# Norm operands built from a gained copy of x, the low parts shared by VectorE and GpSimd

## The reference

```python
def rmsnorm(x, g):
    x32 = x.astype(jnp.float32)
    y = x32 * lax.rsqrt(jnp.mean(x32 * x32, axis=-1, keepdims=True) + EPS)
    return (y * g.astype(jnp.float32)).astype(x.dtype)

for i in range(DEPTH):                       # first block
    h = rmsnorm(x, norm_mix[i])
    x = x + (conformer_conv(h, ...) if i % 2 == 0 else dilated_attention(h, ...))
    h = rmsnorm(x, norm_ffn[i])
    x = x + swiglu(h, w_gate[i], w_up[i], w_down[i])

# second block, both layers: h = _rms_norm(x, norm)*(1+sc)+sh; x = x + g1*(mixer(h) @ w_out)
#                            h = _rms_norm(x, norm)*(1+sc)+sh; x = x + g2*swiglu(h, ...)
```

## Time and profile before

| | |
|---|---|
| time, median of 3 runs | 1299.03 us (1295.66 to 1299.97) |
| the profiled execution | 1299.97 us, of which its span is 1298.6 us |
| PE busy | 1206.4 us, 93% |
| DVE busy | 947.4 us, 73% |
| ACT busy | 659.1 us, 51% |
| POOL busy | 72.9 us, 6% |
| mean granted TensorE clock | 0.976 |

### The profile page before, as it was taken

How to read it: one execution, slowest core, us unless ns; L and a number is a source line. 1 busy time by engine, 2 the same in 40 slices (tenths; PEclk the granted TensorE clock), 3 DMA queues, 4 the chain that set the end, 5 groups by cost and what they waited for, 6 DMA issues and landing times.

```text
span 1298.6 us, 24598 instructions
## 1 busy us (share of the span) xinstructions
PE 1206.4 (93%) x9796; PEld 1149.0 (88%) x9796; DVE 947.4 (73%) x1813; ACT 659.1 (51%) x1142; POOL 72.9 (6%) x82
## 2 busy tenths in 40 slices
PE   5988899999998999999987879999999879999999
PEld 5957899999987999999976758999999767999999
DVE  5966598868777888888796658988885555776652
ACT  6326554445445644446455556444444766544431
POOL 1000000001000100003000011000010112000000
PEclk9999899999999999999998989999999989999999
DMA  8587698778863587778643225877875423555551
GB/s 280 164 193 106 217 306 256 257 261 273 266 184 114 183 270 258 238 269 268 204 147 104 86 93 179 273 253 252 263 261 195 135 90 98 181 187 184 181 193 66
DMA packets 81125, 259.35 MB, mean 200 GB/s; under 512 B 8904, under 2 KB 20424, under 8 KB 81012
## 3 DMA queue, kind: packets, MB, share of 16 engines
q1 hardware_dynamic: 81012, 257.79, 62.3%
HBM read 252.68 MB, written 5.08 MB: 198 GB/s over the span
## 4 chain that ended last, share of the span: by engine, by line
PE 69%; DVE 17%; ACT 5%; issue 4%; DMA 1%; POOL 1%; DVEq 0%; ACTq 0%; POOLq 0%
PE ps L516 63%; DVE wlo L1192 5%; DVE CV L1198 1%; DVE HL L1198 1%; DVE aacc L1198 1%; PE ps L576 1%; DMA raw<-wall 1%; DVE X L1198 1%; ACT oS L834 1%; ACT HH L834 1%; PE ps L607 1%; ACT eS L834 1%; ACT tmp L834 1%; PE ps L615 1%; DVE tmp L1523 1%
## 5 line engine op out<-in xcount | busy, mean ns | idle before, releaser
L516 PE MATMUL ps<-HH,whi 128*128 128x256 f32 (+1 forms) x2152 | 624.2, 290 | 28.4 <-DVE wlo L1192 11.8
L516 PE MATMUL ps<-HH,wlo 128*128 128x256 f32 (+1 forms) x2152 | 614.2, 285 | 0.0
L516 PE MATMUL ps<-HL,whi 128*128 128x256 f32 (+1 forms) x2152 | 613.6, 285 | 0.0
L834 ACT ACTIVATE whi<-raw 128x1024 fp32r<-128x1024 f32 x363 | 381.8, 1057 | 350.0 <-PE ps L516 342.7
L1192 DVE TENSOR_TENSOR wlo<-raw,whi 128x1024 fp32r<-128x1024 f32 x363 | 441.5, 1221 | 44.2 <-ACT whi L834 43.9
L516 PEld LDWEIGHTS ps<-HH,whi 128*128 128x128 f32 x2152 | 414.4, 193 | 46.3 <-issue 29.6
L516 PEld LDWEIGHTS ps<-HL,whi 128*128 128x128 f32 x2152 | 414.4, 193 | 0.9 <-issue 0.5
L516 PEld LDWEIGHTS ps<-HH,wlo 128*128 128x128 f32 x2152 | 413.9, 192 | 0.0
L516 PE MATMUL ps<-GH,whi 128*128 128x256 f32 x704 | 198.1, 281 | 0.6 <-DVE bcol L1405 0.5
L516 PE MATMUL ps<-GH,wlo 128*128 128x256 f32 x704 | 197.5, 281 | 0.0
L516 PE MATMUL ps<-GL,whi 128*128 128x256 f32 x704 | 197.5, 281 | 0.0
(11 more groups left out here) (209 smaller groups left out, 955.2 us busy)
## 6 DMA issues: line engine op xcount, KB each, us to landing
raw<-wall SPq DMA_DIRECT2D x363, 512.0 KB, 4.3
araw<-ada SPq DMA_DIRECT2D x96, 512.0 KB, 4.7
UR<-uscr SPq DMA_DIRECT2D x24, 142.0 KB, 3.3
scratch<-bvec SPq DMA_DIRECT2D x1, 3072.0 KB
oBB<-kbias SPq DMA_DIRECT2D x16, 192.0 KB, 2.6
aTB<-scratch SPq DMA_DIRECT2D x12, 128.0 KB, 2.3
X<-x_in SPq DMA_DIRECT2D x2, 512.0 KB, 5.8
out<-X SPq DMA_DIRECT2D x8, 128.0 KB, 3.0
```

Of the source, the lines that this page charges most:

```text
L516: ins = pe.e.matmul(o, l, r, start=(kt == p.order[0] and i == 0), stop=(kt == p.order[-1] and i == 2))
L834: ac.then_inc(ac.e.activation(o, i, func, **kw), sem)
```

## The change

The product of X and the gain is now written to memory once. DVE computes it as a tensor_scalar into one of three buffers `tn` right after it has updated X (function `gained`, counted by the new semaphore `xg`). ACT rounds that buffer to HH instead of scaling X itself. The low part is `HL <- tn - HH`, a tensor_tensor: on DVE for tiles 0, 2, 4, 6 and 7 (counter `hlv`), on POOL for tiles 1, 3 and 5 (counter `hlp`). DVE's low part stands in the same slot as the X update, where before it stood one slot later. ACT's squares wait for `xg` as well. PE waits for HH and for the counter of the engine that makes the tile's low part.

```diff
-NORM_OF = {1: "pw2", 2: "dn0", 3: "outd", 4: "dn1", 5: "oute", 6: "dn2", 7: "outo"}
+POOL_LOW = (1, 3, 5)
+LOW_NO = {0: 1, 2: 2, 4: 3, 6: 4, 7: 5, 1: 1, 3: 2, 5: 3}
...
+        def norm_low(i, nt):
+            return (S.hlp, 3 * i + LOW_NO[nt]) if nt in POOL_LOW else (S.hlv, 5 * i + LOW_NO[nt])
...
 (PE)            def ready(kt):
-                    pe.wait_ge(S.hl, 8 * i + kt + 1)
+                    pe.wait_ge(S.hh, 8 * i + kt + 1)
+                    pe.wait_ge(*norm_low(i, kt))
...
 (ACT)       def norm_high(i, nt):
-                streamed(i, nt)
+                ac.wait_ge(S.xg, 8 * i + nt + 1)
                 if i:
                     ac.wait_ge(S.mm, end_mm(HH_BEFORE[i]))
-                if i >= 4:
-                    ac.wait_ge(S.gn, 3 if i < 6 else i - 2)
-                act(HH[NORM_SET[i]][:, nt, 0:T], X[:, nt, :], ACT.Copy, S.hh, scale=gain(i, nt))
+                act(HH[NORM_SET[i]][:, nt, 0:T], TN[(8 * i + nt) % 3][:, :], ACT.Copy, S.hh)
             def square(i, nt):
-                streamed(i, nt)
+                ac.wait_ge(S.xg, 8 * i + nt + 1)
...
 (ACT)       def convolution():
-                ac.wait_ge(S.vec, 16)
...
 (DVE)
-            def norm_low(i, nt):
-                dv.wait_ge(S.hh, 8 * i + nt + 1)
-                stt(HL[NORM_SET[i]][:, nt, 0:T], X[:, nt, :], gain(i, nt), HH[NORM_SET[i]][:, nt, 0:T].bitcast(F32),
-                    ALU.mult, ALU.subtract, S.hl)
+            def gained(i, nt):
+                n = 8 * i + nt
+                if n >= 3:
+                    dv.wait_ge(S.hh, n - 2)
+                    dv.wait_ge(*norm_low(*divmod(n - 3, 8)))
+                if i >= 4:
+                    dv.wait_ge(S.gn, 3 if i < 6 else i - 2)
+                ts(TN[n % 3][:, :], X[:, nt, :], gain(i, nt), None, ALU.mult, None, S.xg)
+
+            def norm_lows(i, nt):
+                if nt not in POOL_LOW:
+                    dv.wait_ge(S.hh, 8 * i + nt + 1)
+                    tt(HL[NORM_SET[i]][:, nt, 0:T], TN[(8 * i + nt) % 3][:, :], HH[NORM_SET[i]][:, nt, 0:T].bitcast(F32),
+                       ALU.subtract, S.hlv)
...
 (DVE residual)
                     lows(low_to(name, nt))
-                    if i is not None and nt:
-                        norm_low(i, nt - 1)
                     ps = ended(name, nt)
...
                     stt(X[:, nt, :], ps[:, 0:T], scale(nt), X[:, nt, :], op, ALU.add, S.ev)
+                    if i is not None:
+                        dv.settle()
+                        gained(i, nt)
+                        norm_lows(i, nt)
...
 (DVE convolution)
                 for kt in range(KD):
-                    norm_low(0, kt)
+                    dv.wait_ge(S.x1 if kt >= 4 else S.x0, 16)
+                    gained(0, kt)
+                    norm_lows(0, kt)
...
 (POOL)
+            def norm_lows(i, nt):
+                if nt in POOL_LOW:
+                    po.wait_ge(S.hh, 8 * i + nt + 1)
+                    tt(HL[NORM_SET[i]][:, nt, 0:T], TN[(8 * i + nt) % 3][:, :], HH[NORM_SET[i]][:, nt, 0:T].bitcast(F32),
+                       ALU.subtract, S.hlp)
             def residual(name, i):
                 for nt in range(PROD[name].tiles):
+                    norm_lows(i, nt)
                     added(i, nt)
...
+            for kt in range(KD):
+                norm_lows(0, kt)
             for kt in range(KD):
                 added(0, kt)
```

More of the change, by code:

```diff
@@ L339, in __init__ @@
         self.hi, self.lo, self.mm, self.ev = new("hi"), new("lo"), new("mm"), new("ev")
-        self.hh, self.hl = new("hh"), new("hl")
+        self.xg, self.hh, self.hlv, self.hlp = new("xg"), new("hh"), new("hlv"), new("hlp")
         self.sq, self.sqa, self.tot = new("sq"), new("sqa"), new("tot")
@@ L400, in program @@
         TMP = [sb(f"tmp{i}", [P, T]) for i in range(9)]
-        TN = [sb(f"tn{i}", [P, T]) for i in range(2)]
+        TN = [sb(f"tn{i}", [P, T]) for i in range(3)]
         TS = [sb(f"ts{i}", [P, T]) for i in range(2)]
@@ L436, in program @@
             eBB = [sb(f"eBB{i}", [P, 384], F32, st) for i in range(2)]
-        eOB, eTD = TN, TS[0]
+        eOB, eTD = TN[0:2], TS[0]
         SQC, SQD = sb("SQC", [P, T]), sb("SQD", [P, T])
@@ L1293, in residual @@
                     else:
-                        dv.wait_ge(S.hl, 8 * j + nt + 1)
+                        dv.wait_ge(S.xg, 8 * j + nt + 1)
                     stt(X[:, nt, :], ps[:, 0:T], scale(nt), X[:, nt, :], op, ALU.add, S.ev)
+                    if i is not None:
+                        dv.settle()
+                        gained(i, nt)
+                        norm_lows(i, nt)
                     turned_sums(name, nt)
-                if i is not None:
-                    norm_low(i, p.tiles - 1)
             def convolution():
@@ L1636, in slot @@
                             dv.wait_ge(S.sq2, kt + 1)
-                            dv.wait_ge(S.hl, 8 * 4 + kt + 1)
                             stt(X[:, kt, :], X[:, kt, :], V("fin", kt), RST[0][:, :], ALU.mult, ALU.mult, S.xf)
```

## The result

The changed kernel took 1312.85 us (median of 4 runs, 1306.43 to 1316.91) beside 1299.5 us for the kernel before: 1.0102 times as long, 95% interval 1.0055 to 1.0149. A second set of runs beside the experiments gave 1310.67 us and 1.0098 (1.0075 to 1.0121). Forecast were 1305.4 us and 1300.5 to 1310. The direction was right, the size was not: +6.3 forecast, +11 to +13 measured. The profiled execution took 1311.96 us, its span is 1310.6 us, its mean granted clock 0.971 against 0.976.

The account below looks back on a forecast made before the run. PE was taken to bound the kernel, waiting at products' ends for DVE's last X updates. Start +2.8 and projections +3.5 gave +6.3 us, 1305.4 us for a run like the median; range holding 8 in 10: 1300.5 to 1310.

Parts of the forecast that it names:

- the price of each piece: Whole kernel: DVE's added busy time, +7.9 us, costs nothing in the dn products and everything after them.
- rival 3: Projections' ends: PE's stops grow to 3 us and more, the clock falls, POOL's low parts cost DVE; 1310 us, chance 0.14.
- The projections' +3.5: Ends of pw2, outd, oute, outo: later last X updates, added in full to PE's stops; 2.2 to 5.1 us, middle 3.5.
- the case with all of POOL's work paid by DVE: Projections: POOL's low parts shut out DVE's weight units, some 3 x 0.5 us more a projection; also within rival 3.
- 0.1 a slot: Projections: allowance of 0.1 us a slot for DVE's tensor_scalar being held up by POOL.
- The start: Norm 0: tn, HH and HL delay the squares, reciprocal at 31.2 instead of 28.40; +2.8 us, bounds +2.0 to +3.6.
- rivals 1 and 2: Start and projections: same, start hidden, 1301 to 1303 us, chance 0.19; faster, no POOL interference, 1296 us, chance 0.07.

Follow-up runs that it names:

- e15: The kernel before with only the norms of dn0 and dn1 made the changed way: 1300.11 us, 0.9998 of before.
- e1: The kernel before with only the norm built while dn2 runs made the changed way: 1303.08 us, 1.0024 of before.
- e6: The changed kernel with dn2's last nine modulation steps spread over 17 weight units instead of 13: 1307.11 us, 1.0051 of before.
- e7: The kernel before with dn2's last nine modulation steps spread over 17 weight units instead of 13: 1297.38 us, 0.9974 of before.
- e12: The kernel before with three idle tensor_scalars on DVE ahead of the X update of oute's tile 7: 1302.57 us, 1.0020 of before.
- e14: The kernel before with only the norms of pw2, outd, oute and outo made the changed way: 1307.08 us, 1.0046 of before.
- e13: The kernel before with only norm 0, at the start, made the changed way: 1302.27 us, 1.0018 of before.
- e4: The changed kernel with all eight low parts on DVE and none on POOL: 1319.31 us, 1.0152 of before.

## Why the prediction missed

1. **The failed step** is the sentence in the price of each piece: "in the dn products and everything after them this lies in gaps and costs nothing", with "DVE is never late there" ahead of it. True for dn0 and dn1 (e15, 0.9998). In dn2 DVE's queue is full through tile 4 and ends in the modulation step that PE's sums wait for. The stop there grows from 2.36 to 4.62 us, and the clock falls behind it: together 3.7 to 3.85 us in the traces of the changed kernel against that of before, 3.3 against the mean of the seven traces with the old code, 3.1 alone (e1), 0 in the stretch once the queue has gaps (e6 against e7). I read where PE stands still "beside this change" and looked for X updates as releasers; the stop with aacc as its releaser was in the same timeline.
2. **The clock behind oute** was in rival 3, put at 0.14 and tied to stops of "3 and more". The forecast itself had oute's stop near 3.4, so it met its own rival's condition and gave it no price. The stop came to 2.90 and the clock to 1.5 us (e12, e14); the 2 us of the rival were near. A second fall, behind outo's 2.2 us, costs 0.7 on average; the rival spoke of stops of 3 and more.
3. **The projections' +3.5** was about right. Oute came to +1.6 (+1.1 to +1.9 forecast), outo to +1.6 (+0.4 to +1.5), outd to 0 (+0.3 to +0.8) and pw2, from the reciprocal to its tile 7, to -0.2 to +0.5 (+0.4 to +0.9): some 3.4. That it came out is in part luck, since two terms inside it were off and made up for each other: POOL was second at the weight unit, so the case with all of POOL's work paid by DVE did not come, and the tensor_scalar was caught for 0.57 us in the slots of tiles 4 and 6 of pw2, oute and outo (not in outd), where I had put 0.1 a slot.
4. **The start** was right in its chain: first square 16.58 (16.8), reciprocal 30.92 (31.2), +2.5 for +2.8. PE's first matmul came at 11.60, 0.24 earlier and not 0.6. Its worth was too high: some 1.5 us on average by the traces, 2.3 by e13's ratio (0 to 4.6).
5. **Sum** with the measured terms: start 1.5 to 2.5, projections 3.4, clock behind oute 1.5 and behind outo 0.7, dn2 3.3: 10.4 to 11.4. The parts by themselves give 11.2, the whole 0.0098 x 1300 = 12.7 with 3 us to either side. The misses, dn2 and the clock, are 5.5 us, and forecast plus 5.5 is 11.8.
6. **DVE's busy time** rose from 947.4 to 960.3 us, by 12.9 and not 7.9: it counts what POOL stretched, and the 64 tensor_scalars alone took 0.43 us on average instead of 0.348, 5.2 us more. A low part on POOL took 0.99 us on average against 0.48 on DVE, and e4 shows that the change is worse without it. The forecast's rivals 1 and 2 had no part.

## What to carry to other kernels

Cost more work on an engine at every instruction of it that the bottleneck waits for, not only at those the change is about: list the bottleneck's stops over the whole run with their releasers, and where the releaser's queue has no gap ahead of one, all added work is paid there. A stop has a second price behind it once it is long enough for the clock to fall, here 1.5 to 1.8 us for going from 1.9 to 2.9 us. In a range between, here 2.2 to 2.4 us, one trace doesn't tell whether it is paid: compare several, or a step such as dn2's reads 3.7 where it is 3.3. And look first at what stands ahead of the awaited instruction in its queue: turning it round in the last two slots of four products gave 0.5% with the norm left as it was.

## What the runs showed of the hardware

- A tensor_scalar of 128x256 fp32, one input in SBUF, took 0.35 us alone and 0.92 where a POOL tensor_tensor ran. A POOL tensor_tensor of 128x256 took 0.73 us beside it, 1.10 behind a DVE weight unit and 1.81 when it asked as the unit began.
- POOL that came second cost DVE nothing (the weight unit of 1111.26 took its usual 1.22). The held tensor_scalar and the add beside it show starts 0.03 us apart, 1109.52 and 1109.55, and the same pair met in the slots of tiles 4 and 6 of outo, 5.3 us apart (0.92 and 0.91).
- Behind PE's stop of 2.90 us after oute the granted clock over the next four us was 0.58 (changed), 0.57 (e12) and 0.70 (e14), and 0.57 behind the 4.62 us in dn2. Over the 18 traces it fell behind all 8 stops of 2.87 to 2.91 us after oute and all 7 of 3.5 to 5.6 us in dn2. It fell behind none of the single stops of 1.0 to 1.92 us after outd, oute and outo. Of the 17 single stops of 2.19 to 2.38 us after these three and in dn2 it fell behind 7. (Single: no other stop of 0.95 us or more in the 5 us before.) Behind pw2, where the kernel before stops for 1.91, 1.92 and 1.68 us within 7 us, it was 0.52.
